# A pooling and gated-convolution layer on one Trainium2 core: the four pools computed beside their units, counts made at setup, and another order of tiles in the output product

## What is computed

```python
proj = rms_norm_2(h, norm_mix[0]) @ w_in_even          # 1024 -> 2048
a_b, a_c, a_v, z_b = split(proj, 4)                    # 512 each
y_a = a_b * causal_dwconv3(a_c * a_v, conv_a)
# z_b: four groups of 128 channels, windows 2, 4, 8, 16
for g, w in enumerate((2, 4, 8, 16)):
    count = minimum(arange(1, s + 1), w)
    pooled = (sum of the last w positions of z_g) / count - z_g
    y_b_g = (pooled @ w_pool[g]) * pool_scale_g
h = h + concatenate([y_a, y_b]) @ w_out_even           # 1024 -> 1024
```

## Time and profile before

| what | before |
|---|---|
| median of 3 runs | 2491.84 us (2487.38 to 2496.64) |
| profiled execution: its time | 2490.61 us |
| profiled execution: span | 2489.2 us |
| mean granted TensorE clock | 0.971 of full speed |
| busy share: PE, PEld, DVE, ACT, POOL | 94%, 74%, 57%, 28%, 36% |
| the layer in the trace | about 1437 to 1598 us |

### The profile page before, as it was taken

The page is one execution under the profiler, slowest core; times in us unless marked ns, Lnnn a source line. Parts: engine busy times, 40 slices in busy tenths (PEclk is TensorE's granted clock), DMA queues, the critical chain, the costliest instruction groups (busy, mean ns, idle before and its releaser), DMA issues.

```text
span 2489.2 us, 33880 instructions
## 1 busy us (share of the span) xinstructions
PE 2347.4 (94%) x14398; PEld 1851.1 (74%) x14398; DVE 1424.4 (57%) x1790; ACT 685.3 (28%) x853; POOL 889.0 (36%) x419
## 2 busy tenths in 40 slices
PE   5999999899998799989999988999999999999998
PEld 2777776566666588768888866888888887888887
DVE  3113223577767410666665559788863457888733
ACT  3122112443433322232222221322222332322212
POOL 3422221111110244444444433444444444444442
PEclk8999999899999799979999999999999999999999
DMA  6433332212120333323333313233333322333331
GB/s 216 127 102 111 106 98 78 64 37 51 44 46 10 93 103 99 91 60 102 93 106 101 91 55 102 80 99 102 93 110 94 93 86 84 100 95 96 110 95 56
DMA packets 412039, 222.57 MB, mean 89 GB/s; under 512 B 33823, under 2 KB 409458, under 8 KB 410610
## 3 DMA queue, kind: packets, MB, share of 16 engines
q1 hardware_dynamic: 387394, 208.28, 29.0%
q10 hardware_dynamic: 24496, 12.13, 1.8%
HBM read 214.61 MB, written 5.77 MB: 89 GB/s over the span
## 4 chain that ended last, share of the span: by engine, by line
PE 59%; DVE 6%; issue 0%; ACT 0%; POOL 0%; DVEq 0%; ACTq 0%
PE bank L309 59%; DVE ev_s L2321 0%; PE bank L312 0%; DVE h_low L1929 0%; DVE mg_r_low L1907 0%; DVE g_c L2131 0%; DVE x_res L2278 0%; DVE sq L512 0%; DVE ev_z L2288 0%; DVE sq L508 0%; DVE ev_s L2319 0%; DVE sq L2028 0%; DVE ev_s L2292 0%; DVE ev_low L2333 0%; DVE ev_s L2324 0%
## 5 line engine op out<-in xcount | busy, mean ns | idle before, releaser
L305 POOL TENSOR_TENSOR w_low<-w_raw,w_high 128x1024 fp32r<-128x1024 f32 (+1 forms) x331 | 850.7, 2571 | 1473.1 <-ACT w_high L298 1473.1
L309 PE MATMUL bank<-h_high,w_high 128*128 128x512 f32 x2008 | 809.8, 403 | 38.4 <-DVE h_low L519 20.6
L309 PE MATMUL bank<-h_low,w_high 128*128 128x512 f32 x2008 | 788.9, 393 | 0.0
L298 ACT CAST w_high<-w_raw 128x1024 fp32r<-128x1024 f32 (+1 forms) x331 | 358.5, 1084 | 917.3 <-PE bank L309 899.4
L309 PE MATMUL bank<-h_high,w_low 128*128 128x512 f32 x2008 | 512.5, 395 | 0.0
L309 PEld LDWEIGHTS bank<-h_high,w_high 128*128 128x128 f32 x2008 | 380.2, 189 | 147.4 <-issue 32.9
L309 PEld LDWEIGHTS bank<-h_high,w_low 128*128 128x128 f32 x2008 | 378.7, 190 | 85.0 <-issue 4.6
L309 PEld LDWEIGHTS bank<-h_low,w_high 128*128 128x128 f32 x2008 | 381.1, 190 | 78.1 <-issue 3.4
L309 PE MATMUL bank<-g_high,w_high 128*128 128x512 f32 x352 | 137.9, 392 | 2.3 <-ACT g_c L2110 2.3
L309 PE MATMUL bank<-g_low,w_high 128*128 128x512 f32 x352 | 137.8, 391 | 0.0
L2007 DVE TENSOR_TENSOR x_res<-bank,x_res 128x512 f32<-128x512 f32 x32 | 22.1, 692 | 169.2 <-PE bank L309 169.2
(11 more groups left out here) (368 smaller groups left out, 2888.9 us busy)
## 6 DMA issues: line engine op xcount, KB each, us to landing
w_raw<-in_w_in SPq DMA_DIRECT2D x58, 512.0 KB, 4.6
w_raw<-in_w_up SPq DMA_DIRECT2D x44, 512.0 KB, 3.8
w_raw<-in_w_ffn_gate SPq DMA_DIRECT2D x44, 512.0 KB, 3.8
w_raw<-in_w_ffn_up SPq DMA_DIRECT2D x44, 512.0 KB, 3.8
w_raw<-in_w_ffn_down SPq DMA_DIRECT2D x32, 704.0 KB, 4.4
w_raw<-in_w_ada SPq DMA_DIRECT2D x32, 512.0 KB, 3.8
w_raw<-in_w_down SPq DMA_DIRECT2D x16, 704.0 KB, 4.5
w_raw<-in_w_in ACTq DMA_DIRECT2D x21, 512.0 KB, 4.3
```

Of the source, the lines that this page charges most:

```text
L298: self.A.copy(self.w_high[:, u % SPLIT_SLOTS, 0:k * P], self.raw_of(key)[:, 0:k * P]).then_inc(*self.S.rounded(*key))
L305: self.G.tensor_tensor(self.w_low[:, slot, 0:k * P], self.raw_of(key)[:, 0:k * P], self.w_high[:, slot, 0:k * P].bitcast(F32), ALU.subtrac ...
L309: return self.T.matmul(out, lhsT, rhs, start=start, stop=stop, skip_group_check=True)
```

## The change

1. `plan`, `even_pe`: the load of `w_pool[n]` and the pool's matmul stand ahead of the third unit of block n, no longer behind it.
2. `pool_dve(g)` runs straight behind `ev_zp[g]`. The counts are gone as tiles: only the first `window` columns are multiplied by `window / count`, and the closing product divides by the window and takes the difference in one instruction. The reciprocals of 1 to 16 are made at the kernel's start (four copies of 16 columns by GpSimd, one reciprocal of 64 columns by VectorE).
3. Both roundings to the high part move from VectorE to ScalarE: out of bank 7 with the pool's scale, behind the rounding of the next unit, and of the gated tile n - 1 behind the copy of `c` in block n.
4. The residual tiles are multiplied two by two in the blocks, ahead of the gate's product; the last two after the last low part.
5. The output product takes its tiles in the order 4 to 7, 0 to 3, and its wait for ScalarE's end is gone.
6. In the down projection ahead (where `first` is given), `h_low` is made ahead of the scaling of `x_res` and the second sum of squares.

```diff
@@ plan
             for j in (1, 2, 0):
+                if j == 0:
+                    ring.append((("w_pool", n), [(0, 0, None, io["w_pool_2"][0, n])], None))
                 unit(("even", n, j), even, n * P + j * 4 * P)
-            ring.append((("w_pool", n), [(0, 0, None, io["w_pool_2"][0, n])], None))
@@ product_steps
+        order = self.TILE_ORDER.get(key[0], range(tiles))
-            for k in range(tiles):
+            for k in order:
+    TILE_ORDER = {"even_out": (4, 5, 6, 7, 0, 1, 2, 3)}
@@ setup_pool
+        self.G.iota(self.few_i[:], pattern=[[1, 16]], base=1, channel_multiplier=0).then_inc(*self.S.pool_setup())
+        for g in range(4):
+            self.G.wait_ge(*self.own("pool"))
+            self.G.tensor_copy(self.few[:, g, :], self.few_i[:]).then_inc(*self.S.pool_setup())
@@ rwkv_vectors
+        V.reciprocal(self.few[:], self.few[:]).then_inc(*self.S.dve_ada())
@@ project_pe
-        self.meet("pe", stage, ("act",))
+        if stage != "even":
+            self.meet("pe", stage, ("act",))
@@ project_dve
             if first:
                 self.add_square(self.rinv_first, x)
+                V.wait_ge(*S_.act_norm.at(to, "high", n))
+                low()
+                V.wait_ge(*self.own("dve"))
                 V.tensor_scalar(x, x, first(n), None, ALU.mult).then_inc(*S_.dve_norm())
@@ even_pe
             for m, j in enumerate(self.EVEN_PARTS):
+                if j == 0:
+                    T.wait_ge(*S_.dve_even.at("pooled", n))
+                    T.wait_ge(*self.loaded(("w_pool", n)))
+                    self.empty(7)
+                    self.mm(self.bank[7][:], self.raw_of(("w_pool", n))[:, 0:P], self.e_zp[:, n, :], True,
+                            True).then_inc(*S_.plain_used("w_pool", n))
+                    self.emptied[7] = (S_.dve_even, ("parts", 4 + n))
@@ even_act
                     A.copy(self.e_c[:, n % 2, :], self.even_bank(n, 0)[:]).then_inc(*S_.act_even("c", n))
+                    if n:
+                        self.even_high(n - 1)
+            A.wait_ge(*S_.plain_used.at("w_pool", n))
+            A.activation(self.e_high[:, 4 + n, :], self.bank[7][:], ACT.Copy, bias=0.0,
+                         scale=self.col("pool_scale_2", n)).then_inc(*S_.act_even("high", 4 + n))
+        self.even_high(3)
+    def even_high(self, n):
+        self.A.wait_ge(*self.S.dve_even.at("out", n))
+        self.A.copy(self.e_high[:, n, :], self.e_z[:, n % 2, :]).then_inc(*self.S.act_even("high", n))
@@ even_dve
             V.tensor_tensor(self.e_zp[:, g, :], self.bank[g][:], self.e_root[:], ALU.mult).then_inc(*S_.dve_even("zp", g))
+            self.pool_dve(g)
-            cnt = self.e_cnt[:, g, :]
...
         for n in range(4):
-            self.pool_dve(n)
...
+            V.wait_ge(*S_.act_even.at("high", 4 + n))
+            V.scalar_tensor_tensor(self.e_low[:, 4 + n, :], self.bank[7][:], self.col("pool_scale_2", n),
+                                   self.e_high[:, 4 + n, :].bitcast(F32), ALU.mult,
+                                   ALU.subtract).then_inc(*S_.dve_even("parts", 4 + n))
...
+            if n < 3:
+                self.even_residual(n)
             V.wait_ge(*S_.product.at("even", n, 0))
             V.tensor_tensor(z, c, gate[:], ALU.mult).then_inc(*S_.dve_even("out", n))
-            self.even_parts(n, z)
-            V.wait_ge(*S_.plain_used.at("w_pool", n))
-            V.tensor_scalar(self.e_s1[:], self.bank[7][:], self.col("pool_scale_2", n), None,
-                            ALU.mult).then_inc(*S_.dve_even("mixed", n))
-            self.even_parts(4 + n, self.e_s1[:])
+            V.wait_ge(*S_.act_even.at("high", n))
+            V.tensor_tensor(self.e_low[:, n, :], z, self.e_high[:, n, :].bitcast(F32),
+                            ALU.subtract).then_inc(*S_.dve_even("parts", n))
+        self.even_residual(3)
+    def even_residual(self, n):
+        for k in (2 * n, 2 * n + 1):
+            self.V.tensor_tensor(self.x[:, k, :], self.x[:, k, :], self.rinv_first[:], ALU.mult).then_inc(*self.S.dve_even("residual", k))
@@ pool_dve
-        V.tensor_tensor(src, src, self.e_cnt[:, g, :], ALU.mult).then_inc(*S_.dve_even())
+        V.scalar_tensor_tensor(src[:, 0:window], self.few[:, g, 0:window], float(window), src[:, 0:window], ALU.mult,
+                               ALU.mult).then_inc(*S_.dve_even())
         V.wait_ge(*self.own("dve"))
-        V.tensor_tensor(zp, src, zp, ALU.subtract).then_inc(*S_.dve_even("pooled", g))
+        V.scalar_tensor_tensor(zp, src, 1.0 / window, zp, ALU.mult, ALU.subtract).then_inc(*S_.dve_even("pooled", g))
@@ even_pool
-        self.G.iota(self.e_pos[:], pattern=[[1, S]], base=1, channel_multiplier=0).then_inc(*self.S.pool_setup())
-        self.G.tensor_copy(self.e_posf[:], self.e_pos[:]).then_inc(*self.S.pool_setup("positions"))
```

More of the change, by code:

```diff
@@ L323, in product_steps @@
                 self.T.wait_ge(*self.S.lowered.at(*key))
-            for k in range(tiles):
+            for k in order:
                 if part == "low":
-                    ins = self.mm(out, tile(self.w_low, k), high(k), False, final and k == tiles - 1)
+                    ins = self.mm(out, tile(self.w_low, k), high(k), False, final and k == order[-1])
                     passes += 1
@@ L331, in product_steps @@
                             self.T.wait_ge(*what)
-                    self.mm(out, tile(self.w_high, k), high(k), first and k == 0, False)
+                    self.mm(out, tile(self.w_high, k), high(k), first and k == order[0], False)
                     self.mm(out, tile(self.w_high, k), low(k), False, False)
@@ L2013, in project_dve @@
                 V.tensor_scalar(gained, x, gain(n), None, ALU.mult).then_inc(*S_.dve_norm(to, "gained", n))
+            low = lambda: V.tensor_tensor(self.h_low[:, n, :], gained, self.h_high[:, n, :].bitcast(F32),
+                                          ALU.subtract).then_inc(*S_.h_low_even(to, n))
             if first:
                 self.add_square(self.rinv_first, x)
+                V.wait_ge(*S_.act_norm.at(to, "high", n))
+                low()
+                V.wait_ge(*self.own("dve"))
                 V.tensor_scalar(x, x, first(n), None, ALU.mult).then_inc(*S_.dve_norm())
@@ L2020, in project_dve @@
                 V.tensor_scalar(x, x, gain(n), None, ALU.mult).then_inc(*S_.residual("gained", n))
-            if to:
+            if to and not first:
                 V.wait_ge(*S_.act_norm.at(to, "high", n))
-                V.tensor_tensor(self.h_low[:, n, :], gained, self.h_high[:, n, :].bitcast(F32),
-                                ALU.subtract).then_inc(*S_.h_low_even(to, n))
+                low()
     def add_square(self, total, x, *key):
@@ L2189, in even_layer @@
             self.e_zp, self.e_s1, self.e_s2 = sb("zp", [P, 4, S]), sb("s1", [P, S]), sb("s2", [P, S])
-            self.e_pos, self.e_posf = sb("pos", [P, S], I32), sb("posf", [P, S])
-            self.e_cnt = sb("cnt", [P, 4, S])
             self.e_root, self.e_square = sb("root", [P, S]), sb("square", [P, S])
@@ L2213, in even_pe @@
                 self.emptied[b] = (S_.act_even, ("c", n)) if j == 1 else (S_.dve_even, ("z" if j == 2 else "out", n))
[L2214 to L2219, removed]
         self.end("pe", "even")
@@ L2268, in even_dve @@
             V.tensor_tensor(self.e_zp[:, g, :], self.bank[g][:], self.e_root[:], ALU.mult).then_inc(*S_.dve_even("zp", g))
+            self.pool_dve(g)
         V.tensor_tensor(self.e_square[:], self.e_root[:], self.e_root[:], ALU.mult).then_inc(*S_.dve_even())
-        V.wait_ge(*S_.pool_setup.at("positions"))
-        for g, window in enumerate(POOL_WINDOWS):
-            cnt = self.e_cnt[:, g, :]
[L2273 to L2278, removed]
         for n in range(4):
-            self.pool_dve(n)
             z, c = self.e_z[:, n % 2, :], self.e_c[:, n % 2, :]
@@ L2302, in even_dve @@
             V.tensor_tensor(z, c, gate[:], ALU.mult).then_inc(*S_.dve_even("out", n))
-            self.even_parts(n, z)
-            V.wait_ge(*S_.plain_used.at("w_pool", n))
-            V.wait_ge(*self.own("dve"))
-            V.tensor_scalar(self.e_s1[:], self.bank[7][:], self.col("pool_scale_2", n), None,
-                            ALU.mult).then_inc(*S_.dve_even("mixed", n))
-            self.even_parts(4 + n, self.e_s1[:])
+            V.wait_ge(*S_.act_even.at("high", n))
+            V.tensor_tensor(self.e_low[:, n, :], z, self.e_high[:, n, :].bitcast(F32),
+                            ALU.subtract).then_inc(*S_.dve_even("parts", n))
+        self.even_residual(3)
         self.end("dve", "even")
+    def even_residual(self, n):
+        for k in (2 * n, 2 * n + 1):
+            self.V.tensor_tensor(self.x[:, k, :], self.x[:, k, :], self.rinv_first[:], ALU.mult).then_inc(*self.S.dve_even("residual", k))
     def pool_dve(self, g):
@@ L2340, in even_pool @@
             self.lower_unit(key)
-        self.G.wait_ge(*self.own("pool"))
```

(4 more changed lines are left out.)

## The result

| what | before | changed |
|---|---|---|
| median, 5 runs each | 2491.84 us | 2479.36 us (2472.76 to 2482.02) |
| ratio, 95% interval | | 0.9946 (0.9925 to 0.9967) |
| profiled execution: span | 2489.2 us | 2480.5 us |
| the layer: last add of the down projection to last add of the output product | 159.98 us | 140.05 us |

The gain is 12.5 us (by the ratio's interval 8 to 19) where 19.3 was forecast, and the layer by itself gained 19.9. So the question is not whether the waits went, but where the other 7 to 8 us were lost again.

A forecast was written before the change was run, and what follows sets the result against it. TensorE, busy 94% of the span, bounds the kernel, so only its waits or slow running can be won. Gains of 21.7 less 2.35 given back net 19.3 us: 2472.5 median, range 2466 to 2481.

The forecast's parts named there:

- locks: VectorE instructions with SBUF operands alone, started while GpSimd works, end only 0.5 after it; about 2.4 us each.
- The bound and the places: TensorE busy 94%, so only its waits can be won: layer start, pool 0, and two at the layer's end.
- Part 1: Down projection's last tile: early `h_low` lets the norm's matmuls start at 1445.05, not 1448.84; gain 3.8 us.
- Part 2: Pools beside their units, counts early: pool 0's wait and slow clock go, gain 7.55 us; pool 3's wait, gain 1.63.
- the walk: Step-by-step timing of VectorE's queue, locks included, from `e_root` at 1454.8 to block 0's `out` at 1490.4.
- place 1: Start of the layer: TensorE waits 4.0 us, then takes 3.8 us for ten matmuls before the norm's.
- Part 3: VectorE work moved to ScalarE: unit (1,0)'s rounding queues behind the copy of block 0's `out`; cost 0.4 us.
- Part 4: Output order 4 to 7, then 0 to 3: unit 0 gains 8.7 us without waits; tile 3 costs 0.85.
- the 8.7: Gain in us for unit 0 of the output product without any wait: 14.18 down to 5.49.
- Part 5: Residual tiles 6 and 7 last: first output add 1.4 us late, then 0.6 per unit, none regained; cost 0.6.
- Part 6: Kernel start: GpSimd's small instructions lie beside loads; one 64-column reciprocal on VectorE costs 0.5 us, bounds 0 and 1.
- Late VectorE: Rival, chance 0.15: one more lock of 2.4 us in each of parts 1, 3, 4 and 5, so 2482.

The follow-up runs named there:

- x2: Changed kernel with 192 more bytes behind the two small tiles, so later tiles move by 512 bytes, not 320: median 2471.44 us, layer 139.31.
- x5: Changed kernel with `h_low` again behind the second sum of squares in the down projection: layer 143.52 us against 140.05.
- x6: Changed kernel with each pool's VectorE work back ahead of its own block: layer 155.30 us against 140.05.
- x8: Changed kernel with all eight residual tiles multiplied ahead of block 0 again: layer 143.18 us against 140.05.
- x4: Changed kernel with the output's tiles in the order 0 to 7 again: layer 141.91 us against 140.05.
- x9: Changed kernel with later tiles moved by 960 bytes, plus the reciprocal moved from the kernel's start to the pooling layer's start: median 2467.34 us.
- x10: Changed kernel with late reciprocal and pads putting every big streamed tile 128 bytes past a multiple of 256: median 2466.12 us, ratio 0.9903 to before.

## Why the prediction was right or wrong

**The whole.** The time lay inside the range, but partly by luck: the range left room for locks that did not come, and a loss of another kind, which no part of the sum had, took their place.

**The bound and the places (right).** All waits named went, and every one that came in their place was named. Parts 1 to 5 put the layer's gain at 19.8; it was 19.9, and 20.7 in x2.

**Part 1 (right).** `h_low` starts 2.51 after the last add (1449.95 - 1447.44); the scaling is locked, 2.50 long beside GpSimd's `w_low`, and the norm's matmuls start 7.24 after the add, where 1445.05 - 1437.82 = 7.23 had been said. x5 gives the part 3.5 against 3.8.

**Part 2 (right).** No wait for `ev_zp`. `e_root` came 16.26 after the add and not 17.0: the walk moved it with place 1 alone. That the waits went is shown, but not what each half of the part gave: x6 shows that the earlier matmul needs the pools out of the blocks while VectorE's low part waits for ScalarE, and earlier pools with the matmul in its old place were not run. Nor were the early counts by themselves.

**Part 3 (size a little off).** Block 0's `out` started 50.7 after the add and ended 51.4 after it; the walk had 52.6 (1490.4). So the rounding of unit (1,0) ended at 1500.47 and TensorE came to that unit at 1501.42, and the 0.4 was not paid. x8 shows that the queue was the right thing to watch.

**Part 4 (right).** Tile 3 cost 0.5 where 0.85 was said, and unit 0 of the output otherwise ran through. Of the 8.7, x4 gives the order 1.9; the rest was not taken apart.

**Part 5 (wrong).** The tail behind the last low part is there (`x_res` locked, 3.50 for two tiles), and the first add of the output is 1.4 late as predicted. But the lag does not stay at 0.6 in each unit: the second add follows 4.3 after the first, the third 5.5, and VectorE again waits 0.37 for TensorE from the fourth on. The step that failed is the claim that none of it is regained: behind its lock in unit 0 VectorE finished the unit and began the next before GpSimd's next `w_low` did.

**Part 6 (wrong, and enough for the whole miss of 6.8).** The part counted the instructions that the early counts add at the start: 0.5, which the rows of x9 bear out, with a further cost at the start left open. It did not count the room that they take: the sum has nothing for any stage behind the start and outside the layer. The 320 bytes of the two tiles cost 7.9 by the medians of the changed kernel and x2 (2479.36 and 2471.44); the traces show 2.4, 2.3, 0.8 and 1.8 in the four other stages against the kernel before, of which the 2.4 and the 0.8 are near the scatter, and 0.7 in the layer (140.05 against 139.31). Spacing and count give 9.5. Without it the gain is 20.4, against 19.3 predicted.

**The rivals.** Late VectorE did not happen: no further lock in parts 1, 3 and 4. The measured time, 2479.36, lies near that rival's 2482, but for another reason. Weights were never waited for.

## What to carry to other kernels

Price a wait by walking the queue of the engine that ends it, other engines' locks included; done for each place, that gave the layer's gain to within a microsecond. It holds for a part undone as well: in x6 VectorE waited for ScalarE, ScalarE for TensorE and TensorE for VectorE, by the order of their queues, which the busy times do not tell. A change that adds or removes a small tile also moves every tile behind it, so compare the start-to-start spacing of matmuls in the stages that the diff does not touch, before crediting or blaming the edit. Here placing the streamed tiles a multiple of 256 bytes from the weights took the changed kernel from 2479.36 to 2466.12 (x10, 0.9903 of the kernel before, and the best of the versions timed more than once), with the reciprocal's 0.5 in it; the early `h_low` and the order of tiles, each undone alone, are worth 3.5 and 1.9.

## What the runs showed that had not been expected

- The spacing of these fp32r matmuls (128x128 weights, 512 columns, full clock, no waits) depends on the distance from the weights' to the streamed tile's address modulo 256 bytes: 0.227 at 0, 0.229 at 64, 0.233 at 128 and at 192. Moving the weights' tiles by 64 bytes made the whole kernel 50 us slower (one run).
- An unused tile of 320 bytes made the unchanged kernel slower by 0.19% (0.07 to 0.31%).
- VectorE's instructions with two tiles in SBUF as operands, its scaling by a column (2.50 in place of 0.49) and its rounding to fp32r (2.51 in place of 0.43) are held until GpSimd's `w_low` ends: all 26 sums into `rinv` that started inside one took 2.76 to 3.60 in the changed kernel's trace, against 0.69. Those that read a bank beside one SBUF operand keep their 0.69, and a memset (0.49) and a copy of one column (0.15) are not held either. The Trainium skill (SBUF — State Buffer, two separate sides) calls it an exclusive lock held for a whole instruction; the traces agree, and GpSimd's own instruction grew from 2.40 by at most 0.5.
